# Two attention units in one turn of TensorE's queue, values last, and queries and keys turned into the projection's banks

## What is computed

```python
def banded_attention(q, k, v, max_dist, sink=None):
    s = jnp.einsum('bnqgrd,bnkgd->bngrqk', qb, kb).astype(jnp.float32) * SCALE
    s = jnp.where(mask, s, MASK_VALUE)
    m = jnp.max(s, axis=-1, keepdims=True)
    p = jnp.where(mask, jnp.exp(s - m), 0.0)
    den = jnp.sum(p, axis=-1, keepdims=True)
    ...
    o = jnp.einsum('bngrqk,bnkgd->bnqgrd', (p / den).astype(v.dtype), vb)

def dilated_mixer(h, pos, w_in):
    for gi, (window, dil) in enumerate(DIL_PATTERNS):   # (128, 1), (512, 4), (2048, 16)
        q = partial_rope(...); k = partial_rope(...)
        o, lse = dilated_attention(q, k, v, window, dil)
    w = jax.nn.softmax(jnp.stack(lses, axis=0), axis=0)
    o = jnp.sum(w[..., None] * jnp.stack(outs, axis=0), axis=0)
    return o.reshape(B, S, MIX_WIDTH) * jax.nn.silu(gate)
```

## Time and profile before

| | us |
|---|---|
| median of 3 runs | 1454.95 |
| lowest, highest | 1454.81, 1456.48 |
| profiled execution | 1460.69 |
| its span, first to last instruction | 1458.9 |
| TensorE busy | 1364.8 |
| VectorE, ScalarE, GpSimd busy | 719.7, 639.7, 398.3 |
| mean granted TensorE clock | 0.962 |

### The profile page before, as it was taken

How to read it: one execution, slowest core, us unless ns; L and a number is a source line. 1 busy time by engine, 2 the same in 40 slices (tenths; PEclk the granted TensorE clock), 3 DMA queues, 4 the chain that set the end, 5 groups by cost and what they waited for, 6 DMA issues and landing times.

```text
span 1458.9 us, 24900 instructions
## 1 busy us (share of the span) xinstructions
PE 1364.8 (94%) x8938; PEld 1230.3 (84%) x8938; DVE 719.7 (49%) x2225; ACT 639.7 (44%) x1769; POOL 398.3 (27%) x443
## 2 busy tenths in 40 slices
PE   4899999998699998999999999999999999997996
PEld 4898988986499987989979889888899799984996
DVE  5543544435732524545435654356644456546625
ACT  6344453536611424445336454346443455446011
POOL 2212141420511011221212823206721218311410
PEclk9999999999599998999999999999999999996898
DMA  5011112122435201011121311202310213215522
GB/s 191 12 30 44 30 53 72 41 77 58 138 102 181 87 22 47 12 36 31 27 65 49 86 52 32 58 23 81 93 27 16 59 49 89 56 35 153 135 101 115
DMA packets 101080, 97.32 MB, mean 67 GB/s; under 512 B 30688, under 2 KB 87520, under 8 KB 100960
## 3 DMA queue, kind: packets, MB, share of 16 engines
q1 hardware_dynamic: 100960, 95.73, 22.2%
HBM read 79.46 MB, written 16.25 MB: 66 GB/s over the span
## 4 chain that ended last, share of the span: by engine, by line
PE 60%; issue 4%; DVE 3%; DMA 3%; ACT 3%; POOL 3%; SPq 1%; DVEq 0%; POOLq 0%; ACTq 0%
PE j_bank L1049 40%; PE s_bank L1151 5%; PE o_bank L1184 5%; PE t_bank L1163 4%; PE t_bank L1130 3%; POOL xr L962 1%; DMA mix_dram<-xr 1%; DMA w_raw<-in_w_out 1%; PE s_bank L1049 1%; PE o_bank L1049 1%; POOL xr L969 1%; ACT probs L1265 1%; DMA ks<-coef_dram 0%; DVE w_lo L1437 0%; ACT gate L1320 0%
## 5 line engine op out<-in xcount | busy, mean ns | idle before, releaser
L1049 PE MATMUL j_bank<-w_hi,ht_hi 128*128 128x384 f32 (+1 forms) x1328 | 455.5, 343 | 15.6 <-DVE ht_lo L1506 7.1
L1049 PE MATMUL j_bank<-w_lo,ht_hi 128*128 128x384 f32 (+1 forms) x1328 | 442.9, 333 | 0.0
L1049 PE MATMUL j_bank<-w_hi,ht_lo 128*128 128x384 f32 (+1 forms) x1328 | 442.3, 333 | 0.0
L1265 ACT ACTIVATE probs<-probs,stat 128x256 f32<-128x256 f32 (+1 forms) x512 | 232.3, 455 | 315.7 <-DVE stat L1469 313.1
L923 POOL TENSOR_TENSOR w_lo<-w_raw,w_hi 128x768 fp32r<-128x768 f32 (+1 forms) x60 | 102.3, 1704 | 717.4 <-ACT w_hi L1256 717.4
L1049 PEld LDWEIGHTS j_bank<-w_hi,ht_hi 128*128 128x128 f32 x1328 | 255.2, 192 | 29.2 <-issue 23.7
L1049 PEld LDWEIGHTS j_bank<-w_lo,ht_hi 128*128 128x128 f32 x1328 | 255.2, 192 | 0.0
L1049 PEld LDWEIGHTS j_bank<-w_hi,ht_lo 128*128 128x128 f32 x1328 | 255.0, 192 | 0.0
L1464 DVE CUSTOM_DVE_ANT_0 probs<-s_bank,masks 128x128 f32<-128x128 f32 (+1 forms) x448 | 141.3, 351 | 77.5 <-PE t_bank L1163 64.9
L1151 PE MATMUL s_bank<-ks,qs 128*128 128x256 f32 (+1 forms) x1024 | 172.4, 292 | 4.2 <-DVE ks L1523 3.3
L1151 PEld LDWEIGHTS s_bank<-ks,qs 128*128 128x128 f32 x1024 | 150.2, 196 | 23.8 <-issue 18.7
(11 more groups left out here) (155 smaller groups left out, 1609.9 us busy)
## 6 DMA issues: line engine op xcount, KB each, us to landing
w_raw<-in_w_qkv SPq DMA_DIRECT2D x64, 384.0 KB, 3.3
coef<-coef_dram SPq DMA_DIRECT2D x96, 128.0 KB, 3.0
w_raw<-in_w_gate SPq DMA_DIRECT2D x32, 256.0 KB, 3.4
mix_dram<-xr SPq DMA_DIRECT2D x12, 512.0 KB, 4.2
w_raw<-in_w_out SPq DMA_DIRECT2D x16, 384.0 KB, 3.5
qk<-mix_dram SPq DMA_DIRECT2D x12, 512.0 KB, 4.3
xr<-in_x SPq DMA_DIRECT2D x8, 512.0 KB, 8.2
out<-xr SPq DMA_DIRECT2D x8, 512.0 KB, 2.7
```

The costliest lines, as they stand in the source:

```text
L1049: last = pe.matmul(to, a(x_, kt), b(y_, kt), start=(start and kt == kts[0] and x_ == y_), stop=(stop and kt == kts[-1] and x_ == 1))
L1265: last = act.activation(row, row, ACT.Exp, bias=stat[:, s.t % 2, n, r, j:j + 1], scale=SCALE, accum_out=stat[:, s.t % 2, n, r, 2 + j:3 + j])
```

## The change

TensorE's loop goes over pairs of slots. In a pair it does both scores, both turns, then the fills and pieces of the two slots in alternation (`pair_work`), and then both times_v, of the units two back (`V_BACK` is 2). The other engines follow in pairs: VectorE does both `mask_max`, the odd unit's `empty_turn`, the fills ahead of the first piece (`front_and_rest`), the rest, then the store; ScalarE the even `empty_turn`, those fills, both `exps`, then weight splits, the rest, and mixed tiles last. Fills are written into the piece banks and counted in `PIECE`, all but half 1 of the keys of a by-class step (`fill_ring`). The fills within a step move to slots 0, 1 and 2; query 0 of half 1 of a by-class step from slot 14 to 13. In steps that end a group the pieces move to slots 0, 1, 3, 5, 6, 7, 9, 10 and the gates' to 12 to 15; the last weight splits of every step but a layer's last stand behind the last pair's exps. GpSimd's loop is as before.

```diff
-            _slots.append((JOBS[-1], [0, 1, 3, 4, 6, 7, 8, 9] if _s.ends_group else [0, 2, 4, 6, 8, 10, 12, 14]))
+            _slots.append((JOBS[-1], [0, 1, 3, 5, 6, 7, 9, 10] if _s.ends_group else [0, 2, 4, 6, 8, 10, 12, 14]))
...
-            _slots.append((JOBS[-1], [0, 2, 4, 6] if _s.last else [11, 12, 13, 15] if _layer == 1 else [11, 12, 13, 14]))
+            _slots.append((JOBS[-1], [0, 2, 4, 6] if _s.last else [12, 13, 14, 15]))
...
-FILLS_WITHIN = {1: ("K", 1), 2: ("Q0", 1), 4: ("Q1", 1)}
+FILLS_WITHIN = {0: ("K", 1), 1: ("Q0", 1), 2: ("Q1", 1)}
...
-V_BACK = 3
+V_BACK = 2
...
-        return {10: [("Q0", 0)], 14: [("Q0", 1)], 15: [("K", 0), ("K", 1)]}.get(slot, [])
+        return {10: [("Q0", 0)], 13: [("Q0", 1)], 15: [("K", 0), ("K", 1)]}.get(slot, [])
...
+def pair_work(s, a):
+
+    fills = [("fill",) + key for key in fills_at(s, a) + fills_at(s, a + 1)]
+    pieces = [("piece",) + key for key in SLOT_PIECES.get((s.t, a), []) + SLOT_PIECES.get((s.t, a + 1), [])]
+    if not s.last and by_class(STEPS[s.t + 1]) and a == UNITS - 2:
+        return fills + pieces
+    work = []
+    while fills or pieces:
+        work += fills[:1] + pieces[:1]
+        fills, pieces = fills[1:], pieces[1:]
+    return work
...
+def fill_ring(key):
+
+    return TURN if by_class(STEPS[key[0]]) and key[1:] == ("K", 1) else PIECE
...
-                    for slot in range(UNITS):
-                        score(s, slot)
-                        b, u = unit_before(s, slot, TURN_BACK)
-                        if b:
-                            turn(b, u)
-                        b, u = unit_before(s, slot, V_BACK)
-                        if b:
-                            times_v(b, u)
-                        for key in fills_at(s, slot):
-                            fill(*key)
-                        for key in SLOT_PIECES.get((s.t, slot), []):
-                            piece(key)
...
+                    for a in range(0, UNITS, 2):
+                        pair = (a, a + 1)
+                        for slot in pair:
+                            score(s, slot)
+                        for b, u in [unit_before(s, slot, TURN_BACK) for slot in pair]:
+                            if b:
+                                turn(b, u)
+                        for item in pair_work(s, a):
+                            if item[0] == "fill":
+                                fill(*item[1:])
+                            else:
+                                piece(item[1:])
+                        for b, u in [unit_before(s, slot, V_BACK) for slot in pair]:
+                            if b:
+                                times_v(b, u)
```

More of the change, by code:

```diff
@@ L1376, in _ @@
                     before = None if s.first else STEPS[s.t - 1]
-                    for slot in range(UNITS):
-                        w_hi(SLOT_SPLIT.get((s.t, slot), []))
-                        b, u = unit_before(s, slot, TURN_BACK)
+                    for a in range(0, UNITS, 2):
+                        pair = (a, a + 1)
+                        front, rest = front_and_rest(pair_work(s, a))
+                        if a == 0:
+                            w_hi(SLOT_SPLIT.get((s.t, 0), []))
+                        b, u = unit_before(s, a, TURN_BACK)
@@ L1380, in _ @@
                         if b:
                             empty_turn(b, u)
-                        if slot == SILU_AT and before is not None and before.ends_group:
-                            silu(before)
-                        for key in fills_at(s, slot):
-                            fill_hi(*key)
-                        if s.last and slot == SPLIT_MIX[0] - 1:
+                        for item in front:
+                            fill_hi(*item[1:])
+                        for slot in pair:
+                            exps(s, slot)
@@ new lines, in _ @@
+                        if SILU_AT in pair and before is not None and before.ends_group:
+                            silu(before)
+                        for slot in pair:
+                            if slot > 0:
+                                w_hi(SLOT_SPLIT.get((s.t, slot), []))
+                        for item in rest:
+                            if item[0] == "fill":
+                                fill_hi(*item[1:])
+                            else:
+                                empty_piece(item[1:])
@@ L1394, in _ @@
[L1394 to L1402 removed]
+                        for slot in pair:
+                            if s.last and slot in SPLIT_MIX:
+                                k = SPLIT_MIX.index(slot)
+                                act.wait_ge(mix_back[k % 3], 16 * (layer * 2 + k // 3 + 1))
+                                mix_split(layer, k, mix_in[k % 3])
+                            if slot == (1 if layer == 0 else 3) and before is not None and before.ends_group:
+                                den_exp(before, 0)
+                            if s.last and slot == END_EXP:
+                                den_exp(s, 0)
@@ L1758, in _ @@
                     before = None if s.first else STEPS[s.t - 1]
-                    for slot in range(UNITS):
-                        b, u = unit_before(s, slot, TURN_BACK)
+                    for a in range(0, UNITS, 2):
+                        pair = (a, a + 1)
+                        front, rest = front_and_rest(pair_work(s, a))
+                        for slot in pair:
+                            mask_max(s, slot)
+                        b, u = unit_before(s, a + 1, TURN_BACK)
                         if b:
@@ new lines, in _ @@
+                        for slot in pair:
+                            w_lo(SLOT_SPLIT.get((s.t, slot), []))
+                        for item in rest:
+                            if item[0] == "fill":
+                                fill_lo(*item[1:])
+                            else:
+                                empty_piece(item[1:])
+                        if a == UNITS - 2:
+                            w_lo(SPLIT_BEHIND.get(s.t, []))
+                        b, u = unit_before(s, a + 1, V_BACK)
@@ L1789, in _ @@
                         if b and u % 4 == 3:
                             store_ot(b, u // NB, (u % NB) // 4)
+                        for slot in pair:
+                            if before is not None and before.ends_group:
+                                if slot == (1 if layer == 0 else 3):
+                                    coefs_first(before, 0)
+                                if slot == (2 if layer == 0 else 4):
+                                    coefs_last(before, 0)
+                                if slot == LATE_C:
+                                    coef_copy(before, 0)
+                            if s.last and slot == END_FIRST:
+                                coefs_first(s, 0)
+                            if s.last and slot == END_LAST:
+                                coefs_last(s, 0)
+                            if s.last and slot == END_COPY:
+                                coef_copy(s, 0)
+                            if s.last and slot in SPLIT_MIX:
+                                k = SPLIT_MIX.index(slot)
+                                mix_split(layer, k, mix_in[k % 3])
```

120 lines of the change are left out of this document (51 added, 69 removed).

## The result

The changed kernel takes 1486.72 us (median of 4 runs, 1484.55 to 1487.15), the kernel before 1455.72 us in the same comparison (median of 4). The ratio is 1.021, 95% interval 1.0192 to 1.0228: slower by 31 us. I had forecast slower by 14 us, 1469 us, in a range that ends at 1487. The direction and the eleven waits held; the forecast difference was less than half of what came.

A forecast was written before the change was run, and what follows sets the result against it. TensorE, busy 94% of the span, was taken to bound the kernel. The terms -37 - 8.7 + 3 + 45 + 17 - 5 gave +14 us, added to the 1454.95 us median: 1469 us, range 1448 to 1487.

The forecast's parts named there:

- eleven waits: Fills of half 1 moved earlier make TensorE wait for GpSimd's rotation behind piece 7, 3.8 to 4.4 us each: 45 us lost.
- one excursion for two units: TensorE goes to times_v once per pair of slots, not twice; 118 pairs at 0.31 us: 37 us gained.
- fills of K ahead of by-class steps: At three boundaries fills in piece banks no longer wait for turn banks; with the clock, 8.7 us gained.
- piece 1 waits for piece 0's bank: In the first pair behind a group-ending boundary, 0.5 us exposed in 6 steps: 3 us lost.
- clock behind them: Lower clock level behind 10 of the 11 new rotation waits, 1.7 us each: 17 us lost.
- ends of the layers: Exps go ahead of late mixed-tile splits, so the output projection begins earlier: 5 us gained, between 0 and 10.
- profiled execution to median: The profile's difference of 14 us was added to the median unchanged, so no further difference was forecast.
- Rival (d): Entering times_v from a piece costs double, so the excursion's cost stays: 1484 us, chance 0.08.
- Rival (a): The clock stays up behind the new rotation waits: 1452 us, chance 0.10.
- Part 4: Layer ends: exps before late splits start layer 0's projection 4.5 us earlier, layer 1 keeps its causes; 5 us gained in all.
- Rival (c): First output quarter's store, moved earlier, waits for the mixed tile's DMA in 3 groups, 4.2 us each: 1482 us, chance 0.12.

The follow-up runs named there:

- E8: E5 with layer 1's mixing at slot 6 and 104 pairs going to times_v twice again, split by a piece's last matmul: 1488.04 us, ratio 1.0208.
- E3: Changed kernel with GpSimd leaving out the second half of the rotation of rows 4 to 7, so part of the computation is missing: 1444.85 us, ratio 0.9913.
- E11: Changed kernel with only VectorE's first store of each step of layer 1 one pair of slots later: 1484.65 us, ratio 1.0188.
- E10: E5 with VectorE's first store of each step of layer 1 one pair of slots later: 1422.26 us, ratio 0.9752.
- E2: Changed kernel with the loads of a layer's last two mixed tiles issued ahead of the coefficients' store and loads on SyncE: 1480.3 us, ratio 1.0148.
- E12: E10 with the splits of the mixed tiles at slots 10 to 15 and layer 0's mixing from slot 6: 1424.71 us, ratio 0.9778.
- E5: Changed kernel with the edits of E1 and E2 together: 1440.76 us, ratio 0.9882.
- E1: Changed kernel with the first piece of the pair put ahead of the fills that need the rotation behind piece 7: 1445.33 us, ratio 0.9911.
- E9: E5 with layer 1's mixing at slot 6 and turns of queries and keys back in the turn banks: 1481.79 us, ratio 1.0159.

## Why the prediction was right or wrong

| step | forecast, us | shown, us |
|---|---|---|
| one excursion for two units | -37 | -34 (118 x 0.287, an estimate from E8) |
| fills of K ahead of by-class steps | -8.7 | about -10 (6.5 idle, two falls) |
| piece 1 waits for piece 0's bank | +3 | +2 (six of 0.32) |
| eleven waits for the rotation | +45 | +43.2 |
| clock behind them | +17 | +19.5 |
| ends of the layers | -5 | about +6 |
| profiled execution to median | 0 | +7 |

**One excursion for two units: right.** Steps that nothing else disturbed got shorter by 0.24 us for each pair in layer 0 (83.85 to 81.90 us from first score to first score) and 0.31 us in layer 1 (60.72 to 58.27). The unknown was the entry from a piece. In the profile after it is 0.26 us from the piece's last matmul to times_v (609.90 to 610.16) against 0.17 us between two matmuls of a piece: 0.09 us more, between the two ends I had kept, near the 0.13 I took. Rival (d) is out. What the Trainium skill says (TensorEngine Tiling (Array Packing), Tiling Modes, Key Properties), that changing the tiling mode drains the engine, fits both this 0.09 us and the lone matmul of E8.

**The waits for the rotation: right, and the largest term.** The number (eleven), the places and the sum are within 2 us of the forecast. The third kind took 3.4 us where I had 3.8, the first 3.9 to 4.7 where I had 4.0, the second 3.1 to 4.1 where I had 4.4.

**The clock: right in kind.** All eleven waits were followed by the lower level, where I had allowed one not to be; it held 3.4 us behind eight and 6.8 us behind three, 47.6 us together. What it cost can be read against E3, which has the same order on TensorE and kept its clock behind seven waits: from the first matmul of the fill to the 70th behind it the changed kernel takes 10.60 us at the first wait (from 617.11) and E3 9.01 us (from 611.54), 1.59 us for one stretch of 3.4 us. Over all eleven waits this adds up to 19.5 us (for four of them against a wait of the same kind), and in E11 to 16.5. E11 and E10, which differ by the waits and by the loads' order, agree with that: 62.4 us, less 42.3 us idle, less 4.6 to 6.4 us for the loads, leaves 14 to 16 us. The Trainium skill's warning of idle gaps (TensorE: Matmul & The Clock Gate, Why this matters for your kernels) has all of them lower the clock, and here all eleven did. Rival (a), that the clock stays up, is out for waits of this size; E3 shows that it is open at 1 to 2.3 us.

**The ends of the layers: wrong, and the step that failed.** I wrote that layer 1 "keeps its order of causes". From the first score of its last step to the output projection it took 64.6 us before (1287.00 to 1351.63) and 74.1 us after (1302.53 to 1376.65). Of the 9.5 us more, 3.1 are the eleventh wait and 1.6 its clock; the pairs should have made the step some 1 to 2 us shorter (an estimate), so the end itself cost 6 us or a little more, and E2 shows that 5 to 6 of them are the loads that slipped behind the coefficients on SyncE's queue. Part 4 of the prediction goes through the splits and exps of ScalarE and VectorE and says nothing of the queue that issues the tiles' loads. In layer 0 the last step was 1.9 us shorter, which is the pairs' gain; the 4.5 us that I expected on top did not come. The splits of slots 8 and 9 now wait for a transfer with copies of turns behind them (TensorE idle 6.82 and 5.07 us there, against 3.48 before); that this is the whole reason isn't shown, since moving these splits in E12 won only 1.3 us in that step. Together the ends came out 11 us from the forecast, the largest part of the 17 us by which it missed.

**From the profile to the median: 7 us.** The profiled execution of the kernel before was 5.7 us over its median, that of the changed kernel 2.2 us below its own. The profiles differ by 24 us, the medians by 31. I had carried the difference over unchanged; an execution that lies so far from the median is worth an allowance in the range. Why the two profiled executions lie on different sides of their medians is open.

The rows of the table add up to 34 for a difference of 31. Smaller pieces went the other way: VectorE's wait of 1.48 us in the earlier trace rows made TensorE wait 1.50 us in the kernel before, with a stretch of 3.4 us at the lower clock behind it (from 1056.6 us), and the changed kernel has neither.

**Rival (c)** was given 1482 us and 0.12. The time came out near it, but not by its mechanism: taking the store's wait away won the changed kernel no more than 2 us, within the spread of its runs (E11). It cost E5, where the waits for the rotation were gone, 18.5 us in three steps (E10), 6 us each against the 4.2 I had priced.

## What to carry to other kernels

When a step is moved by a slot, write down its neighbours on every queue that runs the same loop, the one that only issues transfers too: here one constant moved two loads behind a chain that waits. A consumer put right behind its producer's last input costs the whole chain of the slow engine between them; the same fill one piece later cost 0.2 us in all (E1). And when a wait is taken away, look at what it had been hiding: two waits in one step don't add until one of them is gone.

## What was unexpected

Two banks that seemed enough weren't once the units went in pairs: the same turns of queries and keys cost 23.6 us more in the turn banks (E9). After waits of 3.1 to 4.7 us the clock fell each time, 33 of 33 in the profiles of the changed kernel, E2 and E11; after waits of 1.0 to 2.3 us in 4 of 11 (E3), and of two waits of 1.98 us one was followed by the lower level and one was not, so the length of the wait alone doesn't decide it. What else does is left open.
